# Turns of two attention branches on one NeuronCore: combinations placed ahead of row maxima, and the units of two wide tiles interleaved

## Chip, core and metric

One NeuronCore of a Trainium2 chip runs the whole program. The metric is device time in microseconds (us) of one execution; lower is better. PE is TensorE, DVE VectorE, ACT ScalarE, POOL GpSimd, SP the sync engine that issues the DMAs.

## What is computed

Two layers of an encoder trunk over 1024 prompt tokens and 64 sample tokens. In each layer three branches read one input projection. Branch A is a convolution with a gated recurrence. Branch B is attention over the keys that an indexer selects (256 of up to 1088). Branch C is differential attention: two softmax maps per head, the second subtracted with a learned weight. The outline, with names of the reference:

```python
proj = einsum('bld,de->ble', rmsnorm(x, g), w_in)
y_a  = rg_lru(causal_conv(a_x)) * silu(a_g)
y_b  = softmax(where(selected, q @ k.T, -inf)) @ v      # 4 heads of 64
p    = softmax(q2 @ k2.T)                               # 4 heads, 2 maps each
y_c  = rmsnorm((p[0] - lam * p[1]) @ v) * (1 - lam_init)
x    = x + rmsnorm(concat(y_a, y_b * silu(b_g), y_c * silu(c_g)) @ w_out)
```

All of it is float32 (the scores with the queries split in a high and a low part, hence two matmuls for each piece of keys).

## The kernel before

A layer has a front part (input projections, indexer scores, selection of the keys, branch A) and an attention part. In the attention part the queries are cut in nine tiles: tiles 0 to 7 of 128 prompt rows, whose tile t attends to 128(t+1) keys, and tile 8 (`SAMPLE`), with 64 rows and 1088 keys. They are done in the order `ORDER = [7, 8, 6, 0, 1, 2, 3, 4, 5]`. A tile is a list of units, one for each head of a branch (two heads at a time for branch B of the sample tile). In each tile all four units of C stood first, then those of B. `ATT` is the list of all 70 units, `FIRST[n]` the number of the first unit of the n-th tile, `NTH` the tile's place for a unit.

`schedule()` writes one list, `STEPS`, by hand-made rules, and every engine walks through that list and does its own part of each step, in order:

- `qk`: PE writes a score map to one of two PSUM slots, which take turns (`SLOT`); DVE takes its row maximum (L1588) in the same step. PE must wait until the slot's map of two steps ago has been read by `exp`.
- `exp`: ACT, the exponentials with their row sum (L1255).
- `comb`: DVE. In a unit of C it divides by both sums and folds map 1 into map 0 (L636 to L641), and nothing of that unit can be transposed before this is done. In a unit of B it is one reciprocal (L629).
- `tr`: PE transposes four 128x128 blocks of the exponentials into one PSUM bank (L1874); ACT copies them out in C, DVE in B (both L614). Units of tiles 4 to 8 have two or three such groups.
- `pv`: PE, probabilities times values (L1893); `div`: DVE scales the result (L657, L671).
- `ytr`, `proj`, `square`, `rows`: transposing a finished tile's output, its output projection (L1936, a few matmuls per unit: `QUOTA`), the sum of squares, and the post-norm on DVE (L1616), followed by the residual addition on POOL (L1041) and the store.

While unit i is transposed and multiplied, the scores of unit i+1 are made: in `schedule()`, `one` and `two` are the steps of the first and the second map of unit i+1, `own` is unit i's `comb`, `pv` and `div` those of unit i-1, `rows_now` a finished tile's `rows`, `groups` unit i's `tr` steps, `take` gives projections. For tiles with two groups the order in `before` is (L201 and L202):

```python
steps += one[:-1] + ytr + one[-1:] + own + rows_now + two[:-1]
steps += take(i, 1) + groups[:1] + two[-1:] + take(i, quota - 1) + pv + div + groups[1:]
```

Here `one[:-1]` is the `qk` of map 0, `one[-1:]` its `exp`. So a map-0 maximum of unit i+1 stands ahead of unit i's combination on DVE.

The queries of a tile are not used as they lie. POOL splits them into high and low parts (`pad_c`, `pad_b`: L950 and L955 for C, L980 and L985 for B; plain copies for the sample tile), then SP moves halves across partitions (`cross_c` L744, `cross_b` L754). PE waits for these DMAs at a branch's first unit of a tile (`qc_in`, `qb_in`). `PAD_C_AT[n]` is the unit at whose first map the C queries of tile n+1 are made ready; B's are made at the tile's own first unit. The very first tile's (`pad_c(0)`, `pad_b(0)`, `cross_b(0)`) stand ahead of the list; `pad_b(0)` stands behind `tokens_ready(pool)`, a wait for the last four evacuations of the input projections, two of which belong to `LAST_ROWS`: input projections that PE does inside `STEPS`, right behind the first two score maps (L1773, L1766).

## Time and profile before

| what | value |
|---|---|
| median of 3 runs | 1707.88 us (1705.3 to 1713.13) |
| the profiled execution, own time | 1700.6 us |
| its span | 1698.8 us |
| mean granted TensorE clock | 0.975 |
| busy: PE / PEld / DVE / ACT / POOL | 93% / 64% / 67% / 37% / 25% |

The profiled execution is 7.3 us (0.4%) below the median of the runs. The span is what the profiler saw from the first to the last instruction; "own time" is that execution's measured time. Clock figures are shares of 2.4 GHz: 1.00 is that level, 0.50 is 1.2 GHz, and a number between them is a stretch with some of both. The attention part of layer one lies at about 465 to 850 us, that of layer two at 1300 to 1690 us. In it tile 7 takes 475.95 to 521.41 us and 1305.03 to 1353.63 us, from the first instruction behind `LAST_ROWS` to the first score map of the sample tile; tile 6 takes 563.52 to 603.22 us and 1395.73 to 1440.88 us, from its second unit's scores to the first of tile 0.

### The profile page before, as it was taken

Reading aid. Unit: us, or ns where it says so; the run is one execution under the profiler, and the core shown is the slowest. Engines: PE = TensorE matmul, PEld = TensorE weight load, DVE = VectorE, ACT = ScalarE, POOL = GpSimd, SP = SyncE. Lnnn points to the kernel's source line nnn. Section 1 sums busy time; section 2 is a strip of 40 time slices with the busy share of each in tenths; the row PEclk is TensorE's granted clock in tenths of the full one; section 3 lists DMA queues with packets and bytes.
Section 4 is the critical chain, followed back from the end, with each engine's and each line's share of the span. In section 5 each row is a group of like instructions: output and inputs, shape, how many; then the busy total and the mean of one; then the engine's idle time right before and its main releaser. Section 6 shows DMA issues by size and latency. Waiting matters only on the chain. (4 is left out here: it accounts for less than half of the span.)

```text
span 1698.8 us, 21027 instructions
## 1 busy us (share of the span) xinstructions
PE 1579.7 (93%) x7298; PEld 1085.2 (64%) x7298; DVE 1135.0 (67%) x2456; ACT 629.6 (37%) x1227; POOL 429.1 (25%) x540
## 2 busy tenths in 40 slices
PE   6999999999979798989989999999998888999887
PEld 4566566678867665666556666666887767466663
DVE  3478999967955645555345899999487455455551
ACT  3276621218043323433316753212452333233340
POOL 2000620530012244431410043233100212445311
PEclk9999999999989999999999999999999798999999
DMA  5100000321050212111411000113101303111101
GB/s 176 54 22 20 34 25 27 115 70 51 0 184 7 112 32 63 44 38 32 158 56 54 25 25 25 50 56 100 56 26 58 130 9 112 45 50 56 50 12 52
DMA packets 38888, 98.13 MB, mean 58 GB/s; under 512 B 8640, under 2 KB 27584, under 8 KB 34432
## 3 DMA queue, kind: packets, MB, share of 16 engines
q1 hardware_dynamic: 38784, 96.80, 17.2%
q8 instruction: 59, 0.97, 0.2%
q14 instruction: 45, 0.37, 0.1%
HBM read 65.79 MB, written 18.14 MB: 49 GB/s over the span
## 5 line engine op out<-in xcount | busy, mean ns | idle before, releaser
L1697 PE MATMUL ps<-r_xn,r_w 128*128 128x384 f32 (+1 forms) x1728 | 555.6, 473 | 11.8 <-DVE r_xn L1353 6.3
L1697 PEld LDWEIGHTS ps<-r_xn,r_w 128*128 128x128 f32 x1728 | 326.4, 191 | 195.3 <-issue 14.6
L1454 DVE TENSOR_SCALAR_CACHE_REDUCE r_ix<-r_sc,smi 128x768 bf16<-128x768 f32 (+6 forms) x380 | 342.0, 962 | 2.2
L1255 ACT ACTIVATE r_sc<-ps,sm 128x1024 f32<-128x1024 f32 (+8 forms) x204 | 156.1, 765 | 305.8 <-DVE sm L1588 305.4
L1588 DVE TENSOR_REDUCE sm<-ps 128x1 f32<-128x1024 f32 (+8 forms) x204 | 159.7, 786 | 120.3 <-PE ps L1856 55.6
L1773 PE MATMUL ps<-r_w,r_xn 128*128 128x256 f32 x1024 | 223.4, 380 | 0.0
L1773 PEld LDWEIGHTS ps<-r_w,r_xn 128*128 128x128 f32 x1024 | 194.1, 190 | 27.1 <-issue 1.0
L1893 PEld LDWEIGHTS ps<-r_vg,r_w 128*128 128x128 f32 (+1 forms) x1176 | 156.1, 201 | 56.7 <-issue 25.8
L1874 PE MATMUL ps<-ident,r_sc 128*128 128x128 f32 (+1 forms) x684 | 120.4, 287 | 62.6 <-DVE r_sc L641 47.5
L1874 PEld LDWEIGHTS ps<-ident,r_sc 128*128 128x128 f32 (+1 forms) x684 | 85.2, 150 | 133.8 <-issue 102.4
L1893 PE MATMUL ps<-r_vg,r_w 128*128 128x64 f32 (+1 forms) x1176 | 157.4, 280 | 7.5 <-DVE r_w L657 4.9
L1936 PE MATMUL ps<-r_xn,r_ag 128*128 128x512 f32 x256 | 131.7, 613 | 2.7 <-ACT r_vg L1271 2.7
L1936 PE MATMUL ps<-r_xn,r_vg 128*128 128x512 f32 x256 | 132.4, 621 | 0.0
L1416 DVE SCALAR_TENSOR_TENSOR r_sc<-r_vg,sm,r_sc 128x384 f32<-128x384 f32 (+6 forms) x98 | 97.8, 998 | 28.9 <-ACT r_vg L1168 23.4
L657 DVE TENSOR_SCALAR r_w<-ps,sm 128x64 f32<-128x64 f32 x128 | 35.7, 279 | 97.6 <-PE ps L1893 97.1
L614 DVE COPY r_w<-ps 128x512 f32<-128x512 f32 (+3 forms) x104 | 58.9, 566 | 62.9 <-issue 37.8
L1168 ACT ACTIVATE r_vg<-ps 128x384 f32<-128x384 f32 (+6 forms) x112 | 88.5, 795 | 30.0 <-PE ps L1734 23.5
L614 ACT COPY r_w<-ps 128x512 f32<-128x512 f32 (+3 forms) x112 | 55.3, 493 | 100.7 <-PE ps L1874 100.3
L1850 PE MATMUL ps<-kst_c,qc_hi 128*128 128x512 f32 (+3 forms) x192 | 80.3, 419 | 5.2 <-ACT r_sc L1255 3.5
L873 POOL COPY sm<-r_ax 128x3 f32<-128x3 f32 x8 | 4.0, 503 | 266.0 <-ACT r_ax L1107 266.0
L1734 PE MATMUL ps<-iks,iqs 128*128 128x384 f32 (+3 forms) x160 | 68.7, 500 | 1.5 <-ACT iqs L1150 1.5
L1217 ACT ACTIVATE r_ix<-r_sc,smi 128x896 bf16<-128x896 f32 (+2 forms) x60 | 67.1, 1120 | 6.6 <-DVE smi L1495 6.4
(254 smaller groups left out, 2057.3 us busy)
## 6 DMA issues: line engine op xcount, KB each, us to landing
r_w<-w_in SPq DMA_DIRECT2D x28, 1024.0 KB, 5.0
r_xn<-w_out SPq DMA_DIRECT2D x2, 4096.0 KB, 13.4
y<-r_res SPq DMA_DIRECT2D x16, 512.0 KB, 2.9
r_vg<-x SPq DMA_DIRECT2D x8, 512.0 KB, 10.0
r_xn<-ckT SPq DMA_DIRECT2D x2, 2048.0 KB, 8.5
r_xn<-vcache SPq DMA_DIRECT2D x2, 2048.0 KB, 14.2
o_v<-r_vg SPq DMA_DIRECT2D x4, 1024.0 KB, 10.9
r_sc<-x SPq DMA_DIRECT2D x8, 512.0 KB, 4.8
```

Source lines behind the costliest of these rows:

```text
L614: ins = copy(pT[i % 2][:, k0:k1, 0:r], src[:, 0:k1 - k0, 0:r])
L1168: drains_x(nc.scalar.activation(dst, src, ACT.Relu, scale=scale), key)
L1255: ins = nc.scalar.activation(ex[2 * (i % 2) + m][0:r, 0:w], on_slot(("qk", i, m), w, r), ACT.Exp, bias=negm[0:r, c:c + 1], accum_out=den[0 ...
L1416: ins = vec.scalar_tensor_tensor(sc[t][0:r, 0:w], src, iw[0:r, t, h:h + 1], sc[t][0:r, 0:w], ALU.mult, ALU.add)
L1454: ins = vec.tensor_scalar(unsel[t][0:rows(t), :], sc[t][0:rows(t), :], b, None, op, ALU.add, accum_out=cnt[0:rows(t), c:c + 1])
L1588: vec.tensor_reduce(negm[0:r, c:c + 1], on_slot(s, w, r), X, ALU.max, negate=True)\
L1697: ins = nc.tensor.matmul(on_ring(key, cn), w[:, k, P * s:P * (s + 1)], xnT[:, k, c0:c0 + cn], start=(k == 0), stop=(k == KT - 1))
L1773: ins = nc.tensor.matmul(on_ring(key)[:, BW * (t - t0):BW * (t - t0 + 1)], xnT[:, k, P * t:P * (t + 1)], w[:, k, :], start=(k == 0), stop= ...
L1850: ins = nc.tensor.matmul(out, q, kst[kind][:, h, c0:c0 + cn], start=(n2 == 0), stop=(n2 == 1 and not more))
L1874: ins = nc.tensor.transpose(tbank[0:kn, P * (k - 4 * g):P * (k - 4 * g) + r], ex[2 * (i % 2)][0:r, P * k:P * k + kn], ident[0:r, 0:r])
L1893: ins = nc.tensor.matmul(obank[0:r, 0:vals.shape[1]], pT[i % 2][0:kn, k, 0:r], vals, start=(k == 0), stop=(k == nk - 1))
L1936: ins = nc.tensor.matmul(mixb[:, half, :], yk, wo[:, k, BANK * half:BANK * (half + 1)], start=(k == 0), stop=(k == KT - 1))
```

## The change

1. In tile 7 the units alternate, C B C B C B C B. In tile 6 they stand C B C C C B B B. The other tiles keep C C C C B B B B.
2. In tiles with two groups (4 to 7) the combination of a unit of C stands ahead of both maxima of the next unit, and both `exp` steps behind the first transposition's copy. A unit of B keeps its order, except that the second map of a following unit of C comes behind the first group of transpositions.
3. `rows` stands further back: behind the first group in tiles 4 to 7, at the unit's end in tiles 0 to 3.
4. The queries: C of the sample tile is made ready at unit 1, B of tile 6 at unit 10 (in place of 14), C of tile 0 at unit 19 (in place of 18). A wait of the sample tile's C queries goes. Nothing changes for `pad_b(0)` and `cross_b(0)`.

No instruction is added or removed on PE, DVE or POOL; they only stand in another order.

```diff
--- before.py
+++ after.py
@@ -101,10 +101,18 @@
     return 2 if (t, kind) == (SAMPLE, "B") else 4
 
 
-ATT = [(t, kind, h) for t in ORDER for kind in "CB" for h in range(units_of(t, kind))]
+KINDS = {7: "CBCBCBCB", 6: "CBCCCBBB"}
+
+
+def units_in(t):
+
+    kinds = KINDS.get(t, "C" * units_of(t, "C") + "B" * units_of(t, "B"))
+    return [(t, kind, kinds[:i].count(kind)) for i, kind in enumerate(kinds)]
+
+
+ATT = [u for t in ORDER for u in units_in(t)]
 NTH = [ORDER.index(t) for t, _, _ in ATT]
 FIRST = [NTH.index(n) for n in range(NT)] + [len(ATT)]
-FIRST_B = [FIRST[n] + 4 for n in range(NT)]
 
 
 def maps_of(i):
@@ -115,7 +123,7 @@
 
 def last_map(n, kind):
 
-    i = (FIRST_B[n] if kind == "C" else FIRST[n + 1]) - 1
+    i = max(i for i, u in enumerate(ATT) if u[:2] == (ORDER[n], kind))
     return ("qk", i, maps_of(i) - 1)
 
 
@@ -185,7 +193,7 @@
         plain = t == SAMPLE or kind == "B"
         if len(groups) == 1:
             head = one[:-1] + ytr + one[-1:] + own if plain else own + one[:-1] + ytr + one[-1:]
-            steps += head + take(i, 1) + pv + rows_now + two + take(i, quota - 1) + groups + div
+            steps += head + take(i, 1) + pv + two + take(i, quota - 1) + groups + div + rows_now
         elif t == SAMPLE:
             ahead = []
             if i + 2 < len(units) and maps_of(i + 1) == maps_of(i + 2) == 1:
@@ -197,9 +205,12 @@
                 steps += groups[:1] + ahead[:1] + groups[1:2] + pv + groups[2:] + ahead[1:] + div
             else:
                 steps += groups[:1] + two[-1:] + pv + groups[1:] + div
+        elif plain:
+            steps += one[:-1] + ytr + one[-1:] + own + take(i, 1) + groups[:1] + two + rows_now
+            steps += take(i, quota - 1) + pv + div + groups[1:]
         else:
-            steps += one[:-1] + ytr + one[-1:] + own + rows_now + two[:-1]
-            steps += take(i, 1) + groups[:1] + two[-1:] + take(i, quota - 1) + pv + div + groups[1:]
+            steps += own + one[:-1] + ytr + two[:-1] + take(i, 1) + groups[:1] + rows_now + one[-1:] + two[-1:]
+            steps += take(i, quota - 1) + pv + div + groups[1:]
     last = len(units)
     hold[0] = last
     steps += [("pv", last - 1), ("div", last - 1)]
@@ -272,7 +283,8 @@
 STEPS = schedule()
 FRONT = front()
 STACKED = [n for n in range(NT) if ORDER[n] != SAMPLE]
-PAD_C_AT = [FIRST_B[n] if ORDER[n] != SAMPLE else FIRST[n] + 1 for n in range(NT - 1)] + [None]
+PAD_C_AT = [FIRST[n] + 1 if SAMPLE in ORDER[n:n + 2] else last_map(n, "C")[1] + 1 for n in range(NT - 1)] + [None]
+PAD_B_AT = [None] + [FIRST[n] if ORDER[n - 1] != SAMPLE else FIRST[n - 1] + 2 for n in range(1, NT)]
 MAPS = [s for s in STEPS if s[0] == "qk"]
 SLOT = {k: n for n, k in enumerate(MAPS)}
 RINGJOB = {k: n for n, k in enumerate([("fm",) + s[1:4] if s[0] == "mm" else s for s in FRONT + LAST_ROWS
@@ -801,8 +813,9 @@
                             n = NTH[s[1]]
                             if s[1] == PAD_C_AT[n] and n + 1 in STACKED:
                                 cross_c(n + 1)
-                            if s[1] == FIRST[n] and n in STACKED[1:]:
-                                cross_b(n)
+                            for k in STACKED[1:]:
+                                if s[1] == PAD_B_AT[k]:
+                                    cross_b(k)
                         elif s == ("pv", last):
                             sp.wait_ge(o_filled, last + 1)
                             sp.dma_start(wo, w_out[layer]).then_inc(wo_in, 16)
@@ -931,7 +944,6 @@
                         t, r = ORDER[n], rows(ORDER[n])
                         cols = slice(P * t, P * t + r)
                         if t == SAMPLE:
-                            wait_filled(pool, last_map(n - 1, "C"))
                             for g in range(4):
                                 rg = slice(CHALF * g, CHALF * (g + 1))
                                 ins = nc.gpsimd.tensor_copy(qsc[rg, g // 2, :, g % 2, :],
@@ -994,8 +1006,8 @@
                             n = NTH[s[1]]
                             if s[1] == PAD_C_AT[n]:
                                 pad_c(n + 1)
-                            if s[1] == FIRST[n] and n:
-                                pad_b(n)
+                            if s[1] in PAD_B_AT:
+                                pad_b(PAD_B_AT.index(s[1]))
                         if s in deferred:
                             continue
                         if s[0] == "pv":
```

The new file is 12 lines longer ahead of the engines' code, so an instruction of line L1850 before is L1862 after.

The head of tile 7 on PE (L1773, L1766 input projections; `kst_c` C keys, `kst_b` B keys; L1874 transpositions), in the kernel before:

```order
L1773 MATMUL ps<-r_w,r_xn 128x256 [waits ring_drained2,w_ready1]
L1773 MATMUL ps<-r_w,r_xn 128x256 x15
L1766 MATMUL ps<-r_w,r_xn 64x128 [waits ring_drained3,w_ready1]
L1766 MATMUL ps<-r_w,r_xn 64x128 x15
L1850 MATMUL ps<-kst_c,qc_hi 128x512 [waits drained_a]
...
L1856 MATMUL ps<-chunk,diagm 128x128
L1850 MATMUL ps<-kst_c,qc_hi 128x512 [waits drained_b]
...
L1856 MATMUL ps<-chunk,diagm 128x128
L1874 MATMUL ps<-ident,r_sc 128x128 [waits comb_ready]
L1874 MATMUL ps<-ident,r_sc 128x128 x3
L1874 MATMUL ps<-ident,r_sc 128x128 [waits t_drained]
```

and now:

```order
L1785 MATMUL ps<-r_w,r_xn 128x256 [waits ring_drained2,w_ready1]
L1785 MATMUL ps<-r_w,r_xn 128x256 x15
L1778 MATMUL ps<-r_w,r_xn 64x128 [waits ring_drained3,w_ready1]
L1778 MATMUL ps<-r_w,r_xn 64x128 x15
L1862 MATMUL ps<-kst_b,qb_hi 128x512 [waits sel_ready,qb_in,drained_a]
...
L1865 MATMUL ps<-r_ix,diagm 128x512
...
L1865 MATMUL ps<-r_ix,diagm 128x512
L1886 MATMUL ps<-ident,r_sc 128x128 [waits comb_ready]
L1886 MATMUL ps<-ident,r_sc 128x128 x3
L1886 MATMUL ps<-ident,r_sc 128x128 [waits t_drained]
L1886 MATMUL ps<-ident,r_sc 128x128 x3
L1862 MATMUL ps<-kst_c,qc_hi 128x512 [waits drained_b]
```

The first map of B, with its wait on `qb_in`, took the place of the second unit of C, ahead of the first transpositions.

DVE in the middle of tile 4's C units before (L1588 maximum; L636 to L641 combination; L657, L671 `div`):

```order
L636 RECIPROCAL sm<-sm 128x1 [waits drained_b,drained_a]
...
L639 TENSOR_SCALAR sm<-sm 128x1 [waits dve_step]
L641 SCALAR_TENSOR_TENSOR r_sc<-r_sc,sm 128x640 [waits dve_step]
L1588 TENSOR_REDUCE sm<-ps 128x1 [waits drained_b,filled_b]
L657 TENSOR_SCALAR r_w<-ps,sm 128x64 [waits y_ready,t_filled,o_filled]
L671 SCALAR_TENSOR_TENSOR r_w,sm<-r_w 128x64 [waits o_drained]
L1588 TENSOR_REDUCE sm<-ps 128x1 [waits drained_a,filled_a]
L636 RECIPROCAL sm<-sm 128x1 [waits drained_b,drained_a]
```

and now (L1600, L648 to L653, L669, L683):

```order
L648 RECIPROCAL sm<-sm 128x1 [waits drained_b,drained_a,o_drained]
...
L651 TENSOR_SCALAR sm<-sm 128x1 [waits dve_step]
L653 SCALAR_TENSOR_TENSOR r_sc<-r_sc,sm 128x640 [waits dve_step]
L1600 TENSOR_REDUCE sm<-ps 128x1 [waits drained_a,filled_a]
L1600 TENSOR_REDUCE sm<-ps 128x1 [waits drained_b,filled_b]
L669 TENSOR_SCALAR r_w<-ps,sm 128x64 [waits y_ready,t_filled,o_filled]
L683 SCALAR_TENSOR_TENSOR r_w,sm<-r_w 128x64 [waits o_drained]
L648 RECIPROCAL sm<-sm 128x1 [waits drained_b,drained_a]
```

The combination stood between the two maxima, and now stands ahead of both.

DVE in one turn of C and B in tile 7, now (L626 is the copy of transposed blocks of B, L641 B's reciprocal):

```order
L1600 TENSOR_REDUCE sm<-ps 128x1 [waits drained_b,filled_b]
L669 TENSOR_SCALAR r_w<-ps,sm 128x64 [waits o_filled]
L1600 TENSOR_REDUCE sm<-ps 128x1 [waits drained_a,filled_a,o_drained]
L641 RECIPROCAL sm<-sm 128x1 [waits drained_b]
L626 COPY r_w<-ps 128x512 [waits o_filled,t_filled,dve_step]
L1600 TENSOR_REDUCE sm<-ps 128x1 [waits drained_b,filled_b]
L669 TENSOR_SCALAR r_w<-ps,sm 128x64 [waits o_filled]
L683 SCALAR_TENSOR_TENSOR r_w,sm<-r_w 128x64 [waits o_drained]
L626 COPY r_w<-ps 128x512 [waits t_filled]
L648 RECIPROCAL sm<-sm 128x1 [waits drained_b,drained_a]
```

Between two combinations lie three maxima, two copies and two divisions.

## Rows read from the trace of the kernel before

**Rows 1.** The page: busy time of each engine over the span.
```profile
PE 1579.7 (93%) x7298; PEld 1085.2 (64%) x7298; DVE 1135.0 (67%) x2456; ACT 629.6 (37%) x1227; POOL 429.1 (25%) x540
```

**Rows 2.** Stretches of tiles 7 and 6: us, busy per engine, clock, DMA, GB/s.
```profile
475.95:521.41 45.46, 35.91 (x209) 29.24 (x207) 25.11 (x48) 16.87 (x30) 9.86 (x19) 0.85 0.48 171
1305.03:1353.63 48.60, 39.46 (x208) 31.24 (x207) 25.21 (x48) 16.87 (x30) 9.73 (x19) 0.79 0.44 160
...
563.52:603.22 39.70, 31.99 (x219) 25.54 (x219) 24.75 (x55) 15.32 (x29) 13.12 (x21) 1.00 0.33 122
1395.73:1440.88 45.15, 38.38 (x218) 30.67 (x219) 24.85 (x55) 15.33 (x29) 13.31 (x21) 0.85 0.29 107
```

**Rows 3.** Layer one, transpositions of tiles 7; 6; 4 and 5: busy, mean | idle before.
```profile
L1874 PE MATMUL ps<-ident,r_sc 128*128 128x128 f32 x56 | 10.3, 313 | 9.6 <-DVE r_sc L641 8.9 <-ACT r_w L614 0.7
...
L1874 PE MATMUL ps<-ident,r_sc 128*128 128x128 f32 (+1 forms) x50 | 8.1, 277 | 8.5 <-DVE r_sc L641 7.7 <-DVE r_w L614 0.8
...
L1874 PE MATMUL ps<-ident,r_sc 128*128 128x128 f32 x88 | 15.3, 279 | 10.3 <-DVE r_sc L641 7.6 <-DVE r_w L614 2.7
```

**Rows 4.** Timeline of TensorE in tile 7: start, us, what [idle before].
```profile
475.95 0.51 PE L1850 MATMUL ps<-kst_c,qc_hi 128*128 128x512 f32 x1
...
480.38 0.66 PE L1874 MATMUL ps<-ident,r_sc 128*128 128x128 f32 x4 [2.09 <-DVE r_sc L641]
...
487.49 0.63 PE L1874 MATMUL ps<-ident,r_sc 128*128 128x128 f32 x4 [1.51 <-DVE r_sc L641]
...
513.01 0.48 PE L1850 MATMUL ps<-kst_b,qb_hi 128*128 128x512 f32 x1
...
514.48 0.60 PE L1874 MATMUL ps<-ident,r_sc 128*128 128x128 f32 x4
...
517.17 0.48 PE L1850 MATMUL ps<-kst_b,qb_hi 128*128 128x512 f32 x1
...
521.41 1.02 PE L1846 MATMUL ps<-r_xn,r_res 128*128 128x512 f32 x2
```

**Rows 5.** Timeline of GpSimd and of SP's queue: branch B's first queries; landing time.
```profile
476.78 0.85 POOL L980 CAST qb_hi<-r_qk 64x256 fp32r<-64x256 f32 x2 [109.50 <-ACT r_vg L1205]
...
479.27 1.10 SPq L754 DMA_DIRECT2D qb_lo<-qb_lo  x2
...
DMA to landing us min/median/max: 1.9/2.0/2.1
```

**Rows 6.** Groups of instructions, each shape apart: busy, mean ns.
```profile
L1588 DVE TENSOR_REDUCE sm<-ps 128x1 f32<-128x1024 f32 x24 | 29.1, 1219 | 31.6 <-PE ps L1856 19.9 <-PE ps L1853 11.6
...
L614 DVE COPY r_w<-ps 128x512 f32<-128x512 f32 x56 | 38.6, 690 | 30.5 <-PE ps L1874 12.7 <-issue 12.4 <-DVE sm L629 5.0
...
L641 DVE SCALAR_TENSOR_TENSOR r_sc<-r_sc,sm 128x1024 f32<-128x1024 f32 x8 | 10.5, 1318 | 0.3
...
L1255 ACT ACTIVATE r_sc<-ps,sm 128x1024 f32<-128x1024 f32 x24 | 26.7, 1114 | 35.6 <-DVE sm L1588 35.6
```

**Rows 7.** Single microseconds of tile 7: columns as in rows 2.
```profile
479.00:480.00 1.00, 0.00 (x0) 0.00 (x0) 1.00 (x1) 0.73 (x2) 0.24 (x1) 1.00 0.40 95
483.00:484.00 1.00, 1.00 (x4) 0.38 (x4) 0.00 (x0) 0.24 (x1) 0.00 (x0) 0.50 0.89 360
489.00:490.00 1.00, 1.00 (x7) 1.00 (x6) 0.00 (x0) 0.85 (x2) 0.00 (x0) 0.50 1.03 442
```

**Rows 8.** Landing of `w_out` from its issue at 570.8 us.
```profile
DMA to landing us min/median/max: 12.6/12.6/12.6
```

**Rows 9.** Timeline of VectorE and TensorE in tile 4.
```profile
742.37 0.28 DVE L657 TENSOR_SCALAR r_w<-ps,sm 128x64 f32<-128x64 f32 x1 [1.78 <-PE ps L1893]
...
743.99 0.15 DVE L636 RECIPROCAL sm<-sm 128x1 f32<-128x1 f32 x1
...
761.14 1.28 DVE L1616 SCALAR_TENSOR_TENSOR r_res<-ps,sm,r_ix 128x1024 f32<-128x1024 f32 x1
...
763.08 0.33 PE L1874 MATMUL ps<-ident,r_sc 128*128 128x128 f32 x1 [1.40 <-DVE r_w L614]
```

## Prediction

> **What bounds the kernel now.** I read the page first: PE is busy 93% of the span, so it sets the pace, but the other engines are far from idle [rows 1]. PE can gain only where it stands still, or where its clock is low. Next I cut out the stretches that the change touches and read busy time and granted clock of each [rows 2]. Tile 7 takes 45.46 us in layer one and 48.60 in layer two, tile 6 takes 39.70 and 45.15, though the work is the same. The difference is the clock: 0.85 and 0.79 in tile 7, 1.00 and 0.85 in tile 6. A mean of 0.85 between the levels 1.00 and 0.50 means 30% of the time at 1.2 GHz. In tile 6 this was 13.5 us, and PE was busy 6.4 us longer than at full clock (38.38 against 31.99), so a microsecond at the low clock costs 0.47 us. With that rate tile 7 lost 6.4 us of 13.6 low ones in layer one and 9.6 of 20.4 in layer two, and its work at full clock is 29.5 to 29.9 us, say 29.7. Then I asked what ended PE's idle time. In tile 7 all but 0.7 of 9.6 us, in tile 6 7.7 of 8.5, and in tiles 4 and 5 7.6 of 10.3 us, end with the combination L641 on DVE; in tiles 4 and 5 another 2.7 us end with the copy L614 on DVE [rows 3]. The timeline of tile 7 shows both regimes: in C PE waits about 2 us ahead of each unit's transpositions, in B the period is 4.16 us (513.01 to 517.17) with no wait [rows 4]. So PE waits for DVE in C, and DVE has room in B.
>
> **Tiles 4 and 5: combination first, `rows` later.** At 743.99 us DVE starts a combination behind a maximum of the next unit; it had been free from 742.37 + 0.28, and ACT had finished too [rows 9]. The combination can start about a maximum earlier: 0.8 us in tile 4, more in tile 5, which covers the waits there (7.6 us over eight combinations, 0.95 each). I take all 7.6. The maxima it passes come 1.5 us later, and with them two `exp` steps, which in turn free the PSUM slots for the unit behind. Laid out from these times, that `exp` ends just before PE wants the slot, so I count nothing, but the margin is a few tenths. `rows` (1.28 us at 761.14) stood ahead of the copy for which PE waited 1.40 us at 763.08 [rows 9]; behind it, it delays only a division. I take 1.2 us of each of two such waits. Sum: 7.6 + 2.4 = 10.0 us a layer, 20.0 us in both. In tiles 0 to 3 the moved `rows` meets a DVE that waits for other things anyway, and I count 0; the bounds are 0 and 1.5 us a layer.
>
> **Tile 7: turns.** First a new wait. The unit behind `LAST_ROWS` is now B's first, and it needs `qb_in`. POOL starts on these queries at 476.78, when the last evacuation is done; SP issues the last two DMAs from 479.27 on, the second at about 479.9, and it lands 2.0 us later, at 481.9 [rows 5]. PE is ready at 475.95 [rows 4]. In `before` this lay under the units of C; nothing covers it now, since PE takes its list in order and the first transpositions, whose combination would be done, stand behind the map. That is 6.0 us of idle PE per layer, against 2.1 us there before. Behind it comes the first turn. With 1.22 us for a maximum, 1.11 for an `exp` (1.3 with the read of its sum, an estimate), 1.32 for the large step of a combination (1.85 with the small steps ahead of it, an estimate), 0.69 for a copy [rows 6], and 1.47 us for a map of B (513.01 to 514.48) [rows 4], I laid the steps one behind the other from 481.9: the transpositions of C's second unit start at 493.4, with 8.6 us of PE work in these 11.5. Then the turns repeat. The chain is: transposition, `pv`, transposition, C map 0, its maximum, a copy, the maximum of map 1, a division, a copy, the combination. It comes to 10.4 us. PE works 4.16 us of them for B and 4.8 for C (the same with two maps of C, estimated at 1.05 us each, in place of B's 1.47), so some 1.45 us are idle per turn, twice. Idle is thus 6.0 + 2.9 + 2.9 = 11.8 us, more than the 9.6 before. At full clock tile 7 would take 29.7 + 11.8 = 41.5 us: 4.0 us less than in layer one and 7.1 less than in layer two. All of this gain is clock.
>
> So the clock decides. The rows show it at 1.00 while PE is idle at 479, at 0.50 from about 482, and at 0.50 again at 489, behind a wait of only 1.51 us [rows 4, 7]. The 6 us of idleness will surely be paid for in this way, and 1.45 us waits in every turn may be. I take half of the loss of before: 3.2 and 4.8 us. That leaves 0.8 + 2.3 = 3.1 us for both layers. The bounds are a loss of nothing but what follows the first stall (1.5 us a layer, gain 8.1) and the clock of layer two's 20.4 low microseconds in both layers (gain 11.1 - 19.2 = -8.1).
>
> The Trainium skill (TensorE: Matmul & The Clock Gate, HAM oscillation) says that a wait above a certain length lets the clock gate fall back to half rate, and that the burst behind every such wait starts cold. By that rule alone the new stall costs, and the short waits do not. The trace agrees on the long stretch, but shows a fall behind 1.51 us as well. The page's way out is the second case below.
>
> **Tile 6.** Laid out in the same way from 563.52: its first combination no longer waits for a maximum (1.1 us), B's first map fills C's gap, and the C units behind save a maximum each, less waits of 0.2 to 0.8 us for slots. I come to 37.0 us at full clock, 2.7 less than 39.70. In this sum PE meets `w_out` at its first projection: it is issued when the sample tile's last `pv` ends, lands 12.6 us later [rows 8], and the projection now comes early enough to wait about 1 us; that is in the 37.0. Tile 0's queries have three units of B to hide under in place of four, which is enough. Layer two saves 45.15 - 37.0 = 8.1 us at full clock, 4.9 with half of its 6.4 us of clock loss. Sum 7.6 us.
>
> **Sum.** 3.1 + 7.6 + 20.0 + 0 = 30.7 us off 1700.6, the profiled execution's time: 1669.9. The median of the runs stands 0.43% above that execution, so I give 1669.9 x 1.0043 = 1677 us. The moved query work on POOL costs nothing: it falls into the sample tile, where PE has other work.
>
> **Rivals.**
> 1. *The clock holds.* Only what follows the long stall runs low. Gains: 8.1 (tile 7), 2.7 + 8.1 (tile 6), 20.0: 38.9 us, so 1661.7, or 1669 as a median. For it: fewer waits in a row in C. Against: 1.51 us were enough once.
> 2. *The slot takes the combination's place.* In tiles 4 to 6 the later `exp` steps hold the slot, and PE waits for ACT in place of DVE. The 15.2 us of combinations in tiles 4 and 5 are gone and 2 us in tile 6: 30.7 - 17.2 = 13.5, so 1694. For it: the margin is tenths. Against: DVE and ACT have slack in each unit there.
> 3. *The clock goes low for good, and it is slower.* The 6 us stall and the turns' waits keep PE at 1.2 GHz through tiles 7 and 6. At full clock the change would gain 11.1 + 10.8 + 20.0 = 41.9 us, and it starts from 22.4 us lost. It decides at 42 / 0.47 = 89 low microseconds in the four stretches together, 57% of their 157, against 47.5 us of 178.9 before. All of it low would mean 123 us of full-clock work (2 x 29.7 and 2 x 32.0) at 1.89 times its length, 233 us, and some 12 us of stall: 66 us more than 178.9, less 20 of tiles 4 and 5, so about 1754. For it: the long stall is new. Against: behind each low stretch the clock came back at once when PE was dense.
> 4. *The alternation adds nothing and tile 6's gain is eaten* by the late `w_out` or POOL work beside DVE: only tiles 4 and 5 count, less the small slot waits: 8 us or under, within what can be told from no change, 1700 to 1708.
>
> **How the numbers follow.** A measurement of this kernel tells 0.5% (8.5 us) from no change. Forecast 0.45, rival 1 0.22, rival 2 0.15, what lies between them (tile 7 as low as layer two was before: 1677 + 11 = 1688) 0.08, rival 4 0.06, rival 3 0.04. Faster is the sum of the first four: 0.90; same 0.06; slower 0.04. The range takes in rivals 1 and 2 with little beside them: 1664 to 1694.
>
> **What would show it.** Right: PE idle for about 6 us ahead of the first map of B in tile 7, ended by a DMA on `qb`; waits of about 1.5 us in front of C's transpositions behind it, and none in B; in tiles 4 and 5 idle time of L1886 (the old L1874) near zero, from 10.3 us; tile 6 near 37 us in layer one; clock means of tile 7 near 0.9. Wrong: idle time on L1862 that ACT ends (rival 2), clock means of 0.8 or less in tiles 7 and 6 (rival 3), or a first stall much shorter than 6 us.

## The result, and the profile after

The changed kernel takes 1659.0 us (median of 4 executions, 1657.9 to 1664.9); the kernel before, 1710.5 (1705.3 to 1718.5). The ratio is 0.970, 95% interval 0.966 to 0.975: **faster by 3.0%**. The forecast was 1677 with a range of 1664 to 1694. The sign is right, the size is not: the gain is 51 us; the forecast had 31, against its own base of 1707.9. The profiled execution fell from 1700.6 to 1658.5, by 42 us, where the sum had 30.7.

The page of the changed kernel, its busy times and the clock in 40 slices:

```profile
span 1656.7 us, 20993 instructions
...
PE 1555.5 (94%) x7270; PEld 1069.7 (65%) x7298; DVE 1129.2 (68%) x2456; ACT 625.6 (38%) x1227; POOL 430.6 (26%) x540
...
PEclk9999999999999999999999999999999899999999
```

Against [rows 1] DVE, ACT and POOL do what they did, and PE is busy 24 us less. The same matmuls run, so most of those 24 us are clock: its mean rose from 0.975 to 0.989, which is some 48 us less at the low level, worth up to 23 us at the forecast's rate of 0.47. A little may be records, since this trace holds 28 matmul records fewer. The other 18 us of the 42 are idle time.

The stretches of tile 7 (first two rows) and tile 6 after the change, in the columns of [rows 2]:

```profile
477.50:519.34 41.84, 30.75 (x203) 24.62 (x207) 23.91 (x44) 16.22 (x29) 5.04 (x10) 0.92 0.52 186
1289.01:1332.69 43.68, 32.42 (x203) 25.85 (x207) 24.09 (x44) 16.19 (x29) 4.82 (x10) 0.88 0.50 178
561.50:597.49 35.99, 32.55 (x216) 25.71 (x219) 24.25 (x55) 14.79 (x29) 8.55 (x15) 1.00 0.32 125
1374.86:1413.73 38.87, 33.94 (x215) 27.07 (x219) 24.25 (x55) 14.79 (x29) 8.55 (x15) 0.96 0.30 116
```

The timeline of TensorE in tile 7 (start, us, what, [idle before]), ahead of it the last two DMAs of branch B's first queries, and single stretches in the columns of the windows:

```profile
480.73 1.10 SPq L766 DMA_DIRECT2D qb_lo<-qb_lo  x2
...
483.38 0.77 PE L1862 MATMUL ps<-kst_b,qb_hi 128*128 128x512 f32 x1 [5.88 <-issue]
...
495.92 0.63 PE L1886 MATMUL ps<-ident,r_sc 128*128 128x128 f32 x4 [1.51 <-DVE r_sc L653]
...
506.31 0.63 PE L1886 MATMUL ps<-ident,r_sc 128*128 128x128 f32 x4 [1.50 <-DVE r_sc L653]
```
```profile
480.00:483.00 3.00, 0.00 (x0) 0.00 (x0) 0.00 (x0) 0.00 (x0) 1.85 (x5) 0.50 0.37 87
483.00:486.00 3.00, 2.62 (x5) 1.45 (x7) 0.00 (x0) 0.00 (x0) 0.00 (x0) 0.50 0.95 311
486.00:489.00 3.00, 2.33 (x13) 1.73 (x11) 1.22 (x1) 1.89 (x4) 0.00 (x0) 0.86 1.03 431
489.00:492.00 3.00, 3.00 (x23) 2.39 (x21) 2.54 (x4) 1.51 (x3) 0.00 (x0) 1.00 1.05 431
...
1310.00:1311.00 1.00, 1.00 (x7) 1.00 (x7) 0.28 (x1) 0.00 (x0) 0.00 (x0) 0.50 1.08 383
```

The reader sees the forecast stall, 5.88 us ahead of branch B's first map. The trace names no releaser for it ("issue"), but the last DMA on `qb_lo` is issued at about 481.3, these DMAs land 2.0 us later, and PE starts at 483.38. The reader also sees the turn: its period is 10.39 us (495.92 to 506.31), with a wait of 1.50 in it. In layer one the clock is low from 480 to about 486.8, and for the first 3.4 us of that PE stands still and has nothing to lose; at 489 it is back. In layer two only about 2.3 us of the low stretch lie in the stall, and the clock falls a second time at about 1309.7, for 3 us in which PE is busy.

Here is where the 42 us come from. The marks between stretches are the sample tile's first map and the transposition `ytr` of each tile, which stands in the third unit of the next. The column without turns is experiment 2, below. Values are layer one / layer two, worked out from the timelines of TensorE:

```
stretch                                before        changed       without turns
tile 7                                 45.4 / 48.5   41.8 / 43.7   33.9 / 35.5
second half of tile 8, tile 6          73.8 / 79.2   70.1 / 73.0   69.8 / 72.8
tiles 0, 1, 2                          96.2 / 97.1   90.3 / 90.2   90.6 / 90.2
tile 3, start of tile 4                39.3 / 39.3   39.3 / 39.3   39.3 / 40.9
rest of tile 4, tile 5                 78.1 / 79.5   71.8 / 71.9   71.8 / 71.8
```

The gains in both layers are 8.4, 10.0, 12.7, 0.0 and 13.9 us: 45.0. About 3 us were lost outside these stretches, in work that the change does not touch. These are single traces: in a second trace of the changed kernel tile 7 takes 41.9 and 42.0 us.

### The profile page after: what moved, and what is told of

Its sections match the earlier page's. It is cut to its first block and busy times, and to the rows that moved or that the text cites. A ratio compares the mean times of both kernels' runs of the same rounds, so it can differ in the third digit from the quotient of the medians.

```text
span 1656.7 us, 20993 instructions
## 1 busy us (share of the span) xinstructions
PE 1555.5 (94%) x7270; PEld 1069.7 (65%) x7298; DVE 1129.2 (68%) x2456; ACT 625.6 (38%) x1227; POOL 430.6 (26%) x540
## 5 line engine op out<-in xcount | busy, mean ns | idle before, releaser
L1600 DVE TENSOR_REDUCE sm<-ps 128x1 f32<-128x1024 f32 (+8 forms) x204 | 158.1, 784 | 98.1 <-PE ps L1865 41.2
L1905 PEld LDWEIGHTS ps<-r_vg,r_w 128*128 128x128 f32 (+1 forms) x1176 | 148.9, 192 | 48.5 <-issue 25.4
L1905 PE MATMUL ps<-r_vg,r_w 128*128 128x64 f32 (+1 forms) x1176 | 149.8, 271 | 2.3 <-DVE r_w L626 1.2
L1886 PEld LDWEIGHTS ps<-ident,r_sc 128*128 128x128 f32 (+1 forms) x684 | 84.1, 148 | 96.2 <-issue 65.3
L1886 PE MATMUL ps<-ident,r_sc 128*128 128x128 f32 (+1 forms) x684 | 117.0, 281 | 30.5 <-DVE r_sc L653 16.5
L1948 PE MATMUL ps<-r_xn,r_vg 128*128 128x512 f32 x256 | 128.7, 606 | 0.0
L626 DVE COPY r_w<-ps 128x512 f32<-128x512 f32 (+3 forms) x104 | 59.0, 567 | 73.0 <-issue 52.1
L626 ACT COPY r_w<-ps 128x512 f32<-128x512 f32 (+3 forms) x112 | 55.3, 494 | 129.7 <-PE ps L1886 129.3
L669 DVE TENSOR_SCALAR r_w<-ps,sm 128x64 f32<-128x64 f32 x128 | 35.8, 280 | 73.9 <-PE ps L1905 73.7
L1862 PE MATMUL ps<-kst_c,qc_hi 128*128 128x512 f32 (+3 forms) x192 | 76.2, 397 | 5.6 <-ACT r_sc L1267 4.1
L992 POOL CAST qb_hi<-r_qk 64x256 fp32r<-64x256 f32 x32 | 13.1, 409 | 220.5 <-ACT r_vg L1217 219.0
```

The lines of the kernel that those rows point to most:

```text
L626: ins = copy(pT[i % 2][:, k0:k1, 0:r], src[:, 0:k1 - k0, 0:r])
L1600: vec.tensor_reduce(negm[0:r, c:c + 1], on_slot(s, w, r), X, ALU.max, negate=True)\
L1862: ins = nc.tensor.matmul(out, q, kst[kind][:, h, c0:c0 + cn], start=(n2 == 0), stop=(n2 == 1 and not more))
L1886: ins = nc.tensor.transpose(tbank[0:kn, P * (k - 4 * g):P * (k - 4 * g) + r], ex[2 * (i % 2)][0:r, P * k:P * k + kn], ident[0:r, 0:r])
L1905: ins = nc.tensor.matmul(obank[0:r, 0:vals.shape[1]], pT[i % 2][0:kn, k, 0:r], vals, start=(k == 0), stop=(k == nk - 1))
L1948: ins = nc.tensor.matmul(mixb[:, half, :], yk, wo[:, k, BANK * half:BANK * (half + 1)], start=(k == 0), stop=(k == KT - 1))
```

## The experiments

Each kernel was timed in turn with the kernel before on the same chip. Ratios are to that kernel.

**1. The changed kernel again.** 

> The changed kernel once more, as the mark for the three parts that run beside it on the same chip. Theory A (the gain is real PE time, and the forecast fell short because it left half of the old clock loss in place and gave tiles 0 to 3 nothing): a ratio of 0.972 to 0.976 to the kernel before, as the two profiled executions have it (1658.5 / 1700.6 = 0.975), since the profile of the kernel before was a quick execution of that kernel. Theory B (the medians are right, the kernel before varies and its profile happened to be its best): 0.968 to 0.972.

Measured: 1657.9 us, 0.970 (0.967 to 0.974), while 17 executions of the kernel before ran from 1695.6 to 1714.9 with a median of 1711.9. So theory B holds on this point: the profiled execution of the kernel before, 1700.6, was one of its quick ones, and a median of 1711 compares with a median of 1658.

**2. No turns.** The order of combination and maxima and the place of `rows` are the change's; tiles 7 and 6 take all C units first.

```diff
-KINDS = {7: "CBCBCBCB", 6: "CBCCCBBB"}
+KINDS = {}
```

> Combination ahead of the maxima in tiles 7, 6, 4 and 5, rows later, no turns (KINDS empty). By the two traces tiles 0 to 5 gave 12.1 + 14.6 = 26.7 us over the two layers, and these must stay. In tiles 7 and 6 each C unit's combination comes a maximum earlier: PE waited 9.6 and 8.5 us a layer there. Theory A, the turns are needed in tile 7: 3 to 8 us more for both layers, 1666 to 1671 in a profiled execution, ratio 0.980 to 0.984. Theory C, the place of the combination is all that counted and the 5.9 us stall eats what the turns bring: as fast as the changed kernel or faster, ratio 0.975 or below.

Measured: **1638.9 us, 0.959 (0.955 to 0.962)**, 19 us faster than the changed kernel. Theory C holds, and by much more than it asked for. **The turns cost time.** Tile 7 of this kernel in both layers, in the columns of the windows, and what PE waits for at the transpositions in layer one (busy, mean | idle before):

```profile
477.96:511.83 33.87, 29.89 (x205) 24.02 (x207) 23.81 (x45) 16.23 (x30) 8.86 (x19) 1.00 0.64 230
1279.64:1315.13 35.49, 31.51 (x204) 25.33 (x207) 23.81 (x45) 16.22 (x30) 8.86 (x19) 0.95 0.61 219
```
```profile
L1886 PE MATMUL ps<-ident,r_sc 128*128 128x128 f32 x56 | 8.7, 279 | 3.5 <-DVE r_sc L653 2.9 <-ACT r_w L626 0.7
```

The combination's new place alone takes the waits at the transpositions from 9.6 us [rows 3] to 3.5, and with them nearly all of the low clock goes (0.95 in layer two is some 3.5 us at the low level). After that there is little for a turn to fill. Two timeline rows show a C unit among C units:

```profile
485.59 0.63 PE L1886 MATMUL ps<-ident,r_sc 128*128 128x128 f32 x4 [0.80 <-DVE r_sc L653]
...
491.14 0.63 PE L1886 MATMUL ps<-ident,r_sc 128*128 128x128 f32 x4 [0.70 <-DVE r_sc L653]
```

Its period is 5.55 us, and a B unit among B units takes 4.16 (503.43 to 507.59 in this trace). One of each is 9.71 us, where the turn takes 10.39. In the trace of the changed kernel the unit of B gives PE 4.2 us of work while the chain of the C unit behind it needs more: that unit's second map, issued late, ends at 501.17, its maximum runs until 502.97, its `exp` until 504.20, its combination until 506.16.

**3. Turns with the old order of steps.** All of `schedule` is that of the kernel before, the narrow tiles too; `KINDS` and the places of the queries are the change's. The excerpt shows the lines of the wide tiles:

```diff
-            steps += own + one[:-1] + ytr + two[:-1] + take(i, 1) + groups[:1] + rows_now + one[-1:] + two[-1:]
-            steps += take(i, quota - 1) + pv + div + groups[1:]
+            steps += one[:-1] + ytr + one[-1:] + own + rows_now + two[:-1]
+            steps += take(i, 1) + groups[:1] + two[-1:] + take(i, quota - 1) + pv + div + groups[1:]
```

> Units of both branches in turns in tiles 7 and 6 and queries in that order, but the combination behind the maximum and rows at their old places, as in the kernel before. Theory A: tiles 7 and 6 give 18.5 us less the part of the combination (a maximum of 1.2 us in each of two turns, about 2.5 us per tile and layer, 10 in all): 8 us off, 1692 in a profiled execution, ratio 0.995. Theory C: nothing or slightly slower, ratio 1.00 to 1.005. If the ratio is 0.99 or below, the turns alone carry most of the gain of tiles 7 and 6.

Measured: 1736.1 us, 1.016 (1.012 to 1.020). Slower than before by 1.6%, clear of the noise, and by more than either theory had. Tile 7, its window and two rows of TensorE's timeline:

```profile
477.23:534.27 57.04, 37.53 (x203) 29.90 (x207) 25.47 (x47) 16.69 (x29) 3.94 (x10) 0.79 0.38 136
```
```profile
502.36 0.63 PE L1883 MATMUL ps<-ident,r_sc 128*128 128x128 f32 x4 [3.40 <-DVE r_sc L650]
...
516.29 0.63 PE L1883 MATMUL ps<-ident,r_sc 128*128 128x128 f32 x4 [3.17 <-DVE r_sc L650]
```

It takes 57.0 us against 45.4: 19.5 idle, and 37.5 busy for work that takes 29.9 at full clock.

**4. Only `rows` moved**, in the kernel before; in the wide tiles it stands behind the first transpositions, as in the change.

```diff
-            steps += head + take(i, 1) + pv + rows_now + two + take(i, quota - 1) + groups + div
+            steps += head + take(i, 1) + pv + two + take(i, quota - 1) + groups + div + rows_now
...
-            steps += one[:-1] + ytr + one[-1:] + own + rows_now + two[:-1]
-            steps += take(i, 1) + groups[:1] + two[-1:] + take(i, quota - 1) + pv + div + groups[1:]
+            steps += one[:-1] + ytr + one[-1:] + own + two[:-1]
+            steps += take(i, 1) + groups[:1] + rows_now + two[-1:] + take(i, quota - 1) + pv + div + groups[1:]
```

> The kernel before with only the step rows moved behind the first transpositions or the divisions. The forecast counted 2 waits of 1.2 us per layer in tiles 4 and 5 and nothing in tiles 0 to 3: 4.8 us, ratio 0.997. Theory D, that the moved rows is what gave tiles 0 to 3 their 3.8 us in layer one (its old place held DVE between a division and the maxima, which delayed an exp and with it the next transposition): tile 0 to 3 shorter by 3 to 4 us per layer, 10 to 12 us in all, ratio 0.993.

Measured: 1699.3 us, 0.994 (0.992 to 0.997). Theory D holds for the place: tiles 0 to 2 take 90.3 and 90.2 us for 96.2 and 97.1, the whole 12.7 us that the changed kernel gained there. Here is tile 0 in the kernel before, where the division L657 came late behind `rows`, and the same three-microsecond stretches with `rows` moved:

```profile
639.55 0.39 PE L1850 MATMUL ps<-kst_c,qc_hi 128*128 128x256 f32 x1 [1.64 <-ACT r_sc L1255]
...
642.57 0.66 PE L1893 MATMUL ps<-r_vg,r_w 128*128 128x64 f32 x2 [1.53 <-DVE r_w L657]
```
```profile
642.00:645.00 3.00, 2.43 (x7) 1.50 (x7) 2.59 (x7) 0.56 (x2) 2.84 (x3) 0.59 0.30 73
645.00:648.00 3.00, 2.60 (x7) 1.36 (x7) 2.27 (x8) 1.28 (x5) 1.24 (x2) 0.50 0.52 109
```
```profile
642.00:645.00 3.00, 2.39 (x11) 1.07 (x9) 2.93 (x9) 0.46 (x2) 2.70 (x5) 1.00 0.18 44
645.00:648.00 3.00, 2.84 (x14) 1.90 (x15) 2.27 (x7) 0.99 (x6) 3.00 (x2) 1.00 0.18 44
```

Two waits are gone (1.53 and, at 668.50, 0.93 us). The wait of 1.64 us ahead of the first stays (1.67 with `rows` moved), but the clock, which fell to 0.50 where the two lay close together, now holds at 1.00. That makes 2.5 us a layer of waiting, and 3.4 and 4.4 us for the rest, most of it clock. But a projection now waits 1.79 us for `rows` in tile 3, and here the clock fell behind that, so the stretch of tile 3 and the start of tile 4 took 43.0 us for 39.3 in both layers.

**5. Turns in tile 7 that begin with two units of C**, none in tile 6.

```diff
-KINDS = {7: "CBCBCBCB", 6: "CBCCCBBB"}
+KINDS = {7: "CCBCBCBB"}
```

> The changed kernel with turns in tile 7 alone and these begun with two units of C (CCBCBCBB), so that B's first queries have the first C units to hide under. The kernel without turns takes 33.87 and 35.49 us in tile 7 and the changed kernel 41.84 and 43.67, some 8 us more in each layer. Theory E (the uncovered transfer is the cost): the 5.9 us stall goes, tile 7 takes 35 to 37 us, ratio to the kernel before 0.960 to 0.963. Theory F (alternation itself is the cost, since each C unit behind a B unit brings its waits of 1.5 us and with them the low clock): tile 7 stays at 39 us or more, ratio 0.966 or above.

Measured: 1646.6 us, 0.964 (0.960 to 0.967), between the two theories; tile 7 takes 36.6 and 36.5 us. Its timeline:

```profile
483.77 0.76 PE L1862 MATMUL ps<-kst_b,qb_hi 128*128 128x512 f32 x1 [1.88 <-issue]
...
497.17 0.63 PE L1886 MATMUL ps<-ident,r_sc 128*128 128x128 f32 x4 [1.44 <-DVE r_sc L653]
```

The stretch shrinks by 5.3 and 7.2 us. In layer one the stall gives 4.0 of that, and most of the rest is one wait of 1.5 us less: this order has two C units behind a B unit, where the change has three. So of the 8 us that turns cost in tile 7 of layer one about half are queries that this order covers. 2.7 us remain against 33.9, with a stall of 1.88 and waits of 1.4 to 1.5.

**6. Turns in tile 6 alone.**

```diff
-KINDS = {7: "CBCBCBCB", 6: "CBCCCBBB"}
+KINDS = {6: "CBCCCBBB"}
```

> The changed kernel with turns in tile 6 alone. From the traces the stretch that holds tile 6 takes 70.1 and 73.0 us with turns, 69.8 and 72.5 without, so the turns there are worth nothing: as fast as the kernel without any turns, ratio 0.957 to 0.961, tile 7 at 34 to 35.5 us. Rival: turns in tile 6 cost something that tile 7's longer stretch had hidden (queries made ready later, the output weight arriving), ratio 0.964 or above.

Measured: 1639.6 us, 0.959 (0.955 to 0.964), as without any. Within the interval they are worth nothing, and tile 7 carries the cost.

**7. No turns, and `rows` back at its old places**, so that the order of combination and maxima is all that is left.

> The kernel without turns, with rows at its old places: only the order of combination and maxima is left of the change. If the parts add up, tile 0 is as long as before (35 to 36 us between the two projections' first transpositions, against 31.4 with rows moved), tiles 1 and 2 are 1.7 us longer, and tile 3 to 4 has no wait on r_res: 8 to 10 us slower over both layers than the kernel without turns (1639), so 1645 to 1650, ratio 0.963 to 0.967. Rival: in the faster kernel DVE has room and rows costs nothing where it stands, ratio 0.959 as without turns.

Measured: 1652.0 us, 0.966 (0.962 to 0.970), as the adding up said. Tile 0 takes 36.6 and 35.5 us, tile 3 with the start of tile 4 only 37.2. So the combination's order gains 2.1 us there, which the changed kernel gives back, 1.80 us of it by the new wait on `rows`.

**8. The old preparation of queries**, with the steps of experiment 2 (that is, the kernel before with the two new bodies in `schedule` alone).

> The kernel without turns, with the queries prepared at the places of the kernel before and POOL's wait for the last map of tile 7 back: the order of the steps is that of the run without turns (1639, ratio 0.9586), so this is the part of the change left over. The forecast priced the moved query work at nothing. Expected: 1639, ratio 0.957 to 0.961. Rival: the earlier place is what let the faster tiles 7 and 6 meet ready queries; then PE waits for qc or qb ahead of the sample tile or tile 6 and the ratio is 0.963 or above.

Measured: 1642.0 us, 0.961 (0.958 to 0.964), 3 us above experiment 2, with intervals that overlap. No wait on queries appears. The trace has one difference of size, the clock behind the wait for `w_out` in layer two (below). That the query work costs nothing is not contradicted, but 3 us can't be excluded.

**9. `rows` of tile 1 early again**, no turns. The next projection uses the same PSUM buffer, and in the changed kernel it waits:

```profile
711.67 1.28 DVE L1628 SCALAR_TENSOR_TENSOR r_res<-ps,sm,r_ix 128x1024 f32<-128x1024 f32 x1
...
713.00 1.13 PE L1948 MATMUL ps<-r_xn,r_ag 128*128 128x512 f32 x2 [1.80 <-DVE r_res L1628]
```
```diff
+            if late == 2 and width(t) <= 4 * P:
+                rows_soon = [("rows", done)]
...
-            steps += head + take(i, 1) + pv + two + take(i, quota - 1) + groups + div + rows_now
+            steps += head + take(i, 1) + pv + rows_soon + two + take(i, quota - 1) + groups + div + rows_now
```

> The kernel without turns, but in tile 3 rows of tile 1 stands ahead of the maxima again, since the next tile's projection goes to the same PSUM buffer and waited 1.79 us for it in each layer. Expected: that wait gone, 3.6 us less than without turns, 1635 us, ratio 0.9565. Rival: the wait comes back on the division or the maxima behind rows (1.28 us on DVE), gain below 1 us, ratio 0.9586.

Measured: 1636.7 us, 0.958 (0.954 to 0.961). The stretch fell to 37.2 us in both layers and the wait is gone, 2.1 us a layer. The medians, 1638.9 and 1636.7 from two sessions, can't tell this from no gain.

**10. `rows` at the end of the unit in tiles 4 and 5**, on top of experiment 9. In the changed kernel a division took ten times its usual 0.22 us:

```profile
749.29 1.27 DVE L1628 SCALAR_TENSOR_TENSOR r_res<-ps,sm,r_ix 128x1024 f32<-128x1024 f32 x1
749.42 0.33 PE L1886 MATMUL ps<-ident,r_sc 128*128 128x128 f32 x1 [0.20 <-DVE r_w L626]
...
750.64 2.34 POOL L1053 TENSOR_TENSOR r_res<-r_res,r_sc 128x1024 f32<-128x1024 f32 x1 [3.75 <-DVE r_res L1628]
750.79 2.27 DVE L683 SCALAR_TENSOR_TENSOR r_w<-r_w 128x64 f32<-128x64 f32 x1
752.99 0.28 DVE L626 COPY r_w<-ps 128x128 f32<-128x128 f32 x1
...
753.33 0.66 PE L1886 MATMUL ps<-ident,r_sc 128*128 128x128 f32 x4 [1.59 <-DVE r_w L626]
```
```diff
-            steps += one[:-1] + ytr + one[-1:] + own + take(i, 1) + groups[:1] + two + rows_now
-            steps += take(i, quota - 1) + pv + div + groups[1:]
+            steps += one[:-1] + ytr + one[-1:] + own + take(i, 1) + groups[:1] + two
+            steps += take(i, quota - 1) + pv + div + groups[1:] + rows_now
```

> As split, and in tiles 4 and 5 rows stands at the end of the unit, behind the division and the last copy. In the traces the division's L683, 0.22 us elsewhere, takes 2.27 us when it falls beside POOL's L1053 of 2.34 us, which follows rows, and PE then waits 1.59 us for the copy behind it. Theory G (the two engines hinder each other): L683 stays at 0.22, no wait of 1.59 us in tile 4, 3 us less in both layers than split, 1632 us, ratio 0.9547. Rival: POOL's step meets another instruction of DVE or the projection waits for rows instead: no gain or up to 3 us slower than split.

Measured: 1634.8 us, 0.957 (0.953 to 0.960). The same steps in its trace:

```profile
738.95 0.23 DVE L689 SCALAR_TENSOR_TENSOR r_w<-r_w 128x64 f32<-128x64 f32 x1
...
742.96 2.36 POOL L1059 TENSOR_TENSOR r_res<-r_res,r_sc 128x1024 f32<-128x1024 f32 x1
```

Theory G holds for tile 4: apart from POOL's step the division takes 0.23 us, the 1.59 us wait is gone (a projection now waits 0.62 us for `rows`), and the stretch behind the start of tile 4 is 1.1 us shorter. In tile 5 the late `rows` costs 1.0, so next to nothing is left in sum, where 3 us were expected; the medians, 1636.7 and 1634.8, don't differ beyond their intervals.

**11. The first projection a unit later**, on top of experiment 9.

```diff
-FIRST_PROJ = 3
+FIRST_PROJ = 4
```

> As split, but the first projection one unit later (FIRST_PROJ 4 for 3), so that PE does not meet the wait for the output weight: 1.1 to 2.7 us in layers one and two, behind which the clock fell to 0.50 for some 8 us in one trace (2.69 us of waiting) and not in others (1.97, 2.56). Expected: the wait gone, tile 6 1.2 us shorter in layer one, 2.0 in layer two, no low clock behind it: 3 us less than split, about 1633, and less scatter between executions. Rival: the projections put off by a unit pile up and tile 0 or 1 grows by as much: no gain.

Measured: **1628.4 us, 0.954 (0.950 to 0.958)**, the fastest with the next. The wait for `w_out` is gone, and from tile 7 to the last `ytr` both layers take the same time, 326.8 us. The gain over experiment 9 is 0.4% of the kernel before in ratios, twice what was expected, and the two intervals overlap. The stretch of tile 3 and the start of tile 4 grew from 37.2 to 38.1 us, so a part of the rival's price was paid.

**12. All that helped in one:** no turns, experiments 9 and 11, and `rows` at the end of the unit in tile 4 alone.

> All that helped in one kernel: no turns, combination ahead of the maxima, rows of tile 1 ahead of the maxima of tile 3, rows at the end of the unit in tile 4 alone (there it saved 1.1 us a layer, in tile 5 it cost 1.0), first projection a unit later. The parts add: 1636.7 less 3 (first projection) less 2.2 (tile 4) gives 1631, ratio 0.954 to 0.955.

Measured: 1629.9 us, 0.954 (0.950 to 0.958). No different from experiment 11 within the interval, though the trace has the 1.1 us a layer in tile 4. Both beat the changed kernel, 0.954 against 0.970, by about 28 us.

## Why the prediction was wrong

**Tile 7, idle time: right.** The text had a stall of 6.0 us, a chain of 10.4 us and 1.45 us of waiting in a turn, 11.8 us in all. Measured: 5.88, 10.39, 1.50, and 41.84 - 30.75 = 11.1. The wait of 1.5 us came three times, the first of them in the first turn, for which the text had 2.9 us of idleness; that turn has 0.68 + 1.51 = 2.2.

**Tile 7, "half of the loss of before": mis-sized.** It reckoned with a loss of 3.2 and 4.8 us. PE was busy 30.75 and 32.42 us for work that the text puts at 29.7 us at full clock, so the loss was 1.0 and 2.7 (0.9 and 2.5 against the 29.89 of experiment 2). The gain was 8.4 us, not 3.1. The amount of low clock was as forecast: half of 13.6 and 20.4 us would be 6.8 and 10.2, and the means of 0.92 and 0.88 are 6.7 and 10.5 us at the low level. Its price was not. The text took the 6 us stall as something that "will surely be paid for", at 0.47 us for each low one, but that rate had been read where PE was busy. Here 3.4 us of the low ones in layer one, and 2.3 in layer two, lay in the stall, while PE stood still anyway. The other low ones at 0.47 would still make 1.6 and over 3 us, so the size of the loss is known to about a microsecond.

**Tile 6: nearly right.** 7.6 forecast, 10.0 measured. In layer one 37.0 was forecast and 35.99 measured; layer two kept little of its clock loss (0.96). Experiment 6 shows that the turns had no part in this gain, though the text lets B's first map fill C's gap; the combination's place has it all. The wait for `w_out` is 1.55 us there and none in layer one.

**"In tiles 0 to 3 ... I count 0": this is the term that failed most.** It was 12.7 us, against an upper bound of 3.0. The step asked whether DVE had time for `rows`. It didn't ask what stands behind `rows` on DVE: a division for which PE waits. Nor did it read the clock of tile 0, 0.50 behind waits of 1.64 and 1.53 us. Experiment 4 shows that the whole gain is that move, and experiment 7, with `rows` back, gives the old lengths again (97.2 and 96.1 us).

**Tiles 4 and 5: too large**, 20.0 forecast, 13.9 measured. The combination's waits did go (7.6 us a layer to 0.2). But two things that the text did not look at took a part back. The first is who waits for `rows` itself: the projection's wait of 1.80 us is new, and with it the start of tile 4 gained nothing where experiment 7 gains 2.1 us a layer. The second is what runs on POOL behind `rows`. 2.4 us a layer were booked for the copy's waits. In tile 4 of the kernel before the copy did stand behind `rows`, as the text says, and the division behind that ran beside POOL's step:

```profile
762.34 0.68 DVE L614 COPY r_w<-ps 128x512 f32<-128x512 f32 x1
...
763.25 1.69 DVE L671 SCALAR_TENSOR_TENSOR r_w<-r_w 128x64 f32<-128x64 f32 x1
```

With `rows` moved, that copy's wait fell from 1.40 us [rows 9] to 0.20. But the division now took 2.27 us, the next copy stood behind it, and PE waited 1.59 us for that one (experiment 10): the wait changed its place. In tile 5 the 1.2 us came (experiment 4: 34.6 for 35.8). The two together, 2.1 and 1.2 us a layer, make 6.6 us, about the 6.1 that are missing.

**Outside the stretches** about 3 us were lost that no term had. The sum of the differences is 5.3 + 2.4 + 12.7 - 6.1 - 2.9 = 11.4 us, which is 1669.9 - 1658.5.

**"So I give 1669.9 x 1.0043": the other 7 us.** The factor carried the distance between the median and one quick execution of the kernel before over to a kernel that no longer has it. Executions of the kernel before lie 24 us apart over all measurements, those of the changed kernel 4 to 7. The two layers of one trace show the same: 45.4 against 48.5 us in tile 7 before, by clock alone; in experiment 4's trace the same steps of tile 7 take 42.0 and 48.2. That the changing clock makes the scatter was not shown: experiment 11 has two equal layers in its trace, and its executions still lie 8 us apart.

**The rivals.** The first, that the clock holds, gave 1661.7 for the profiled execution and 1669 as a median and comes nearest. Its parts for tiles 7 and 6, 8.1 and 10.8 us, fit the measured 8.4 and 10.0; that its total does too is luck, since 20.0 for 13.9 in tiles 4 and 5 and 0 for 12.7 in tiles 0 to 3 are wrong in opposite directions. The second did not occur: in neither layer did PE wait for an `exp` in tiles 6, 4 and 5. Nor did the third and fourth. The fourth's 8 us or under does not follow from the text's own 20.0 for tiles 4 and 5 either. But rival 3's stall was the right suspect: turns do cost time, 19 us, and the verdict was faster because the other parts gain 73 us in the same comparison (1711.9 to 1638.9).

**What the text never worked out** is that comparison. It priced tile 7 with turns and the new order together, 41.5 us at full clock, against the old kernel, and called the difference the turns' gain. With the new order alone tile 7 takes 33.9. The parts of the change are: combination ahead of maxima, 0.966; `rows` moved, 0.994 alone; turns, 1.016 with the old order, and 0.970 against 0.959 with the new one.

## What to carry to other kernels

Price each part of a change against the kernel that has all the other parts, not only against the old one; a part that fills a gap is worth nothing once another part has closed it. For a step that moves, ask three things: what was queued behind it, who waits for its result, and what its follower on another engine will run beside. And where waits of 1 to 3 us let the clock fall now and then, a removed wait is worth more than its own length, and the median of several executions, not one profile, is the base of the sum.

## What the runs showed of the hardware

**The same wait, the clock falling or not.** PE waits for `w_out` in layer two. Without turns it waited 2.56 us, and with `rows` back 2.69 us. The windows right behind, first without turns, then with `rows` back:

```profile
1377.00:1380.00 3.00, 0.44 (x4) 0.31 (x3) 2.03 (x2) 0.38 (x1) 1.61 (x1) 1.00 0.16 45
1380.00:1383.00 3.00, 3.00 (x24) 2.49 (x23) 0.20 (x1) 1.59 (x3) 0.00 (x0) 1.00 0.13 34
```
```profile
1386.00:1389.00 3.00, 1.57 (x5) 1.07 (x6) 0.61 (x1) 0.00 (x0) 0.20 (x1) 0.89 0.14 36
1389.00:1392.00 3.00, 3.00 (x16) 3.00 (x16) 0.00 (x0) 1.59 (x3) 0.00 (x0) 0.50 0.04 11
1392.00:1395.00 3.00, 3.00 (x11) 2.08 (x11) 0.52 (x3) 0.48 (x1) 0.00 (x0) 0.50 0.00 0
```

The clock stayed at 2.4 GHz in one and was at 1.2 GHz for some 7 us in the other, which made that stretch 3.3 us longer. It fell as well behind 2.33 us (experiment 10) and 2.79 (experiment 8), and not behind 1.97 (experiment 9). So the length of the wait alone doesn't decide: behind 2.33 it fell and behind 2.56 it didn't. What does decide stays open. The Trainium skill (TensorE: Matmul & The Clock Gate, HAM oscillation) has the burst behind a long wait start cold. The 5.88 us stall agrees: its burst starts at 0.50. The falls behind 2.33 to 2.79 us, and behind the two waits of 1.64 and 1.53 us in tile 0, are behind shorter waits than that rule names.

**VectorE held up by GpSimd.** A 128x64 step of DVE with two SBUF inputs took 2.27 us beside POOL's 128x1024 addition of 2.34 us, and 0.22 elsewhere. The Trainium skill (GPSIMD Engine Reference, Key points) says that GpSimd shares its SBUF interfaces with VectorE and contends with instructions that have two SBUF inputs. The trace agrees: ten times the duration, at the same place in both layers of every kernel that had the two side by side. The step ends when POOL's does: at 753.06 us against 752.98 in the changed kernel, and at 764.94 against 764.85 in the kernel before, where it began later and took 1.69.
